# One section for the output projection and the feed-forward of a hybrid attention block, on one Trainium2 core

## The reference

```python
h = rms_norm(x, norm_mix_pre); proj = h @ w_in
out_a = swa_sink_attention(...)            # sliding window, 512 columns
out_b = diff_attention(...)                # two softmax maps, 512 columns
mixed = jnp.concatenate([out_a, out_b], axis=-1) @ w_out
x = x + rms_norm(mixed, norm_mix_post)
h = rms_norm(x, norm_ffn_pre)
f = (jax.nn.silu(h @ w_gate) * (h @ w_up)) @ w_down      # inner width 2816
x = x + rms_norm(f, norm_ffn_post)
```

## Time and profile before

| | us |
|---|---|
| median of 3 executions (2592.71 to 2597.39) | 2595.13 |
| the profiled execution | 2592.32 |
| its span, first to last instruction | 2590.5 |
| PE busy in the span | 2384.5 |
| output projection, first DMA to last hop store issued | 1054.9 to 1299.6 |
| feed-forward, first DMA to the end | 1307.7 to 2590.5 |

### The profile page before, as it was taken

The page is one execution under the profiler, slowest core; times in us unless marked ns, Lnnn a source line. Parts: engine busy times, 40 slices in busy tenths (PEclk is TensorE's granted clock), DMA queues, the critical chain, the costliest instruction groups (busy, mean ns, idle before and its releaser), DMA issues. The chain is left out here.

```text
span 2590.5 us, 36663 instructions
## 1 busy us (share of the span) xinstructions
PE 2384.5 (92%) x11796; PEld 1979.3 (76%) x11796; DVE 1630.0 (63%) x3093; ACT 1203.6 (46%) x2731; POOL 678.1 (26%) x810
## 2 busy tenths in 40 slices
PE   7999997996898888699769999999999999999998
PEld 5888886885777677577558888888888888888886
DVE  5676776554888888433365555556776655554877
ACT  5555564332666666433343333334554333334444
POOL 1223222221566566354401111110000111111001
PEclk9999998997999999899989999999999999999999
DMA  5111122444232221446463323247675333326774
GB/s 175 48 52 50 47 87 67 132 133 155 69 104 71 76 86 37 161 163 222 163 227 113 103 94 114 82 138 245 195 264 195 107 101 106 113 75 221 245 269 146
DMA packets 222105, 340.08 MB, mean 131 GB/s; under 512 B 20320, under 2 KB 119648, under 8 KB 220128
## 3 DMA queue, kind: packets, MB, share of 16 engines
q1 hardware_dynamic: 221920, 337.86, 39.2%
HBM read 234.50 MB, written 103.28 MB: 130 GB/s over the span
## 5 line engine op out<-in xcount | busy, mean ns | idle before, releaser
L2410 PE MATMUL ff_psum<-ff_hop,ff_a_hi 128*128 128x512 f32 x1760 | 542.4, 389 | 4.3 <-issue 4.3
L2410 PEld LDWEIGHTS ff_psum<-ff_hop,ff_a_hi 128*128 128x128 f32 x1760 | 330.0, 188 | 74.4 <-issue 5.9
L2410 PE MATMUL ff_psum<-ff_hop,ff_a_lo 128*128 128x512 f32 x880 | 342.4, 389 | 0.0
L2434 PE MATMUL ff_psum<-ff_a_hi 128*128 128x512 f32 x616 | 239.6, 389 | 0.0
L2434 PE MATMUL ff_psum<-ff_a_lo,ff_a_hi 128*128 128x512 f32 x616 | 239.6, 389 | 0.0
L2434 PE MATMUL ff_psum<-ff_a_hi,ff_a_lo 128*128 128x512 f32 x616 | 239.6, 389 | 0.0
L2073 ACT ACTIVATE ff_a_hi<-ff_w_raw 128x512 fp32r<-128x512 f32 x220 | 138.0, 629 | 212.8 <-PE ff_psum L2410 190.7
L2410 PE MATMUL ff_psum<-hop,ff_a_hi 128*128 128x512 f32 x704 | 219.0, 392 | 17.0 <-DVE ff_a_lo L2186 17.0
L1222 ACT ACTIVATE da_probs<-da_psum,da_bias 128x512 f32<-128x512 f32 (+3 forms) x320 | 195.9, 621 | 74.0 <-DVE da_bias L1274 60.8
L2186 DVE TENSOR_TENSOR ff_a_lo<-ff_w_raw,ff_a_hi 128x512 fp32r<-128x512 f32 x220 | 161.6, 737 | 104.5 <-ACT ff_a_hi L2073 104.5
L2030 POOL TENSOR_TENSOR ff_go<-ff_go 128x512 f32<-128x512 f32 x22 | 28.4, 1290 | 682.8 <-DVE ff_go L2267 682.8
(11 more groups left out here) (235 smaller groups left out, 5350.9 us busy)
## 6 DMA issues: line engine op xcount, KB each, us to landing
g_s<-ff_go SPq DMA_DIRECT2D x154, 256.0 KB, 2.0
ff_ring<-g_s SPq DMA_DIRECT2D x154, 256.0 KB, 2.7
ff_ring<-in_w_down_dram SPq DMA_DIRECT2D x132, 256.0 KB, 3.1
ff_w_raw<-in_w_gate_dram SPq DMA_DIRECT2D x44, 512.0 KB, 3.6
ff_w_raw<-in_w_up_dram SPq DMA_DIRECT2D x44, 512.0 KB, 3.8
pp_x<-in_x_dram SPq DMA_DIRECT2D x32, 512.0 KB, 4.5
hop_s<-op_ht SPq DMA_DIRECT2D x8, 1792.0 KB, 7.5
ff_hop<-hop_s SPq DMA_DIRECT2D x10, 1024.0 KB, 9.2
```

Of the source, the lines that this page charges most:

```text
L2410: last = pe.matmul(ps[:, bank, :], w[:, unit % R, at], hop[i][:, h, c, :], start=(i in (0, 1, 6) and c == 0 and x_ == 0), stop=(c == 3 and ...
L2434: last = pe.matmul(ps[:, bank, :], g[:, unit % R, at], w[:, (unit + 1) % R, :], start=(i in (0, 1, 6) and c == 0 and x_ == 0), stop=(c == ...
```

## The change

`out_proj` and `ffn` become one function, `out_proj_and_ffn`, with one block and no barrier between the two. `OutProj` holds the steps of the output projection, `TailMap` gives every buffer of both a fixed address. Pieces of the two are interleaved by hand:

- SP loads the first four feed-forward weight pieces after k = 8, ACT and DVE split units 0 and 1 after k = 12, DVE makes the sums x = 1, 3, 2 of round 0 after k = 13, and ACT and DVE split units 2 to 5 (on DVE 2 to 4, with the sums x = 4) in tile 15.
- PE runs up-products 0 and 1 straight behind the last `multiply`, then `turn_h(14)`, products 2 to 4, `turn_h(15)`. The rest of the chains of the tiles 14 and 15 stands between the splits of the feed-forward in the same way.
- The hops 2 to 6 lie where buffers of the output projection lay, so their loads wait: 2 and 3 for the last `multiply`, 4 and 5 for `turn_h(15)` and stores, 6 for the last odd store.
- The hop buffer `op_ht` becomes two even ones and one odd one. Even tiles store two blocks, odd tiles five. The two squares share one junk row. The ring of raw output-projection weights has 8 places, not 6.
- The banks of PSUM in the feed-forward swap halves. The `s` buffer becomes four.
- In the phases `pp` and `da`, tensors of 2048 elements or more per partition start at a multiple of 512 bytes; the old rule was 128. All later ones move up by 384 to 1152 bytes.

```diff
-        align = 128 if size >= 128 else 32
+        align = 512 if size >= 2048 else 128 if size >= 128 else 32
```

On SP, within the loop over k and behind it:

```diff
+            if 1 <= k < TILES - 1:
+                (self.store_even if k % 2 == 1 else self.store_odd)(sp, k - 1)
...
+                def between(k):
+                    if k == 8:
+                        sp.wait_ge(op.w_lo_done, 2 * KC)
+                        for u in range(2):
+                            for v in range(2):
+                                load_raw(0, 0, v, u)
+
+                op.sync(sp, between)
+                sp.wait_ge(op.multiplied, 2 * TILES)
+                load_hop(0, 2)
+                load_hop(0, 3)
+                op.store_x(sp, end)
                 for u in range(2):
                     for v in range(2):
                         load_raw(0, 1, v, u)
-                for i in (5, 6):
-                    load_hop(0, i)
+                op.store_even(sp, end - 1)
+                sp.wait_ge(op.h_turned, 2 * TILES)
+                for n in range(2):
+                    sp.wait_ge(op.x_stored[n], 16 * TILES // 2)
+                sp.wait_ge(op.even_stored[0], 32 * TILES // 4)
+                load_hop(0, 4)
+                load_hop(0, 5)
+                op.store_odd(sp, end)
+                sp.wait_ge(op.even_stored[1], 32 * TILES // 4)
+                sp.wait_ge(op.odd_stored, 16 * TILES // 2)
+                load_hop(0, 6)
```

On ACT:

```diff
+                        if n_ == 2:
+                            act.wait_ge(op.multiplied, 2 * end + 1)
...
+                def between(k):
+                    if k == 12:
+                        hi_until(1)
+                    if k == end:
+                        hi_until(5)
...
+                        if p == 0 and g == 2:
+                            hop_half(0, 2, 1)
+                            op.copy_h(act, end - 1)
+                        if p == 0 and g == 5:
+                            op.copy_h(act, end)
                         up_slot(p, j, q)
                         hi_until(UNITS * p + g + 6)
-                        if p == 0 and g in (2, 4, 6, 8, 10):
+                        if p == 0 and g == 1:
+                            hop_half(0, 2, 0)
+                            op.square_x(act, end)
+                        if p == 0 and g in (4, 6, 8, 10):
```

On DVE, and then on PE:

```diff
+                def between(k):
+                    if k == 12:
+                        lo_until(1)
+                    if k == 13:
+                        for x in (1, 3, 2):
+                            for v in range(2):
+                                s_of(0, 0, x, v)
+                    if k == end:
+                        lo_until(3)
+                        for v in range(2):
+                            s_of(0, 0, 4, v)
+                        lo_until(4)
...
+                        if p == 0 and g == 3:
+                            op.norm_x(dve, end)
...
+                            if p == 0 and j == 0 and q in (1, 4):
+                                op.turn_h(pe, end - 1 if q == 1 else end)
```

More of the change, by code:

```diff
@@ L1733 @@
-class FfnMap:
-    def __init__(self, nc, hops):
-        def at(name, shape, offset, dt=F32):
-            return nc.alloc_sbuf_tensor_at(f"ff_{name}", shape, dt, offset=offset)
-        def area(n):
-            return FFN_BASE + AREA * n
-        self.hop = list(hops) + [at(f"hop{n}", [P, 2, 4, HT], area(n), F32R) for n in range(2, 7)]
-        self.keep = at("keep", [P, FC // 2, HT], area(0))
-        self.y_back = at("y_back", [P, 4, D], area(2))
-        self.x_back = at("x_back", [P, 4, D], area(3))
-        self.x_in = at("x_in", [P, 4, D], area(4))
-        self.y2 = at("y2", [P, 4, D], area(5))
-        self.y1 = at("y1", [P, 4, D], area(6))
-        off = area(7)
-        self.w_raw = at("w_raw", [P, 2, 2, 2, D], off)
-        self.ring = at("ring", [P, 16, HT], off)
-        off += 32768
-        self.s1 = at("s1", [P, 2, HT], off)
-        off += 4096
-        self.a_hi = at("a_hi", [P, 7, HT], off, F32R)
-        off += 14336
-        self.a_lo = at("a_lo", [P, 7, HT], off, F32R)
-        off += 14336
-        self.s = at("s", [P, 4, HT], off)
-        off += 8192
-        self.go = at("go", [P, 7, HT], off)
-        off += 14336
-        self.post_row = at("post_row", [P, D], off)
-        off += 4096
-        self.junk = at("junk", [P, D], off, BF16)
-        off += 2048
-        self.half = at("half", [P, 4], off)
-        self.ss = at("ss", [P, 2, 4], off + 32)
-        self.rstd = at("rstd", [P, 4], off + 64)
@@ L1776, in ffn, with out_proj_and_ffn @@
+def out_proj_and_ffn(nc, x, swa_t, mixed, w_out, subln, g_mix, g_ffn, hop_s, x_mid, g_s, y_s, w_gate, w_up, w_down,
+                     g_post, out):
     PAIRS = 2
@@ L1798, in ffn @@
     with ExitStack() as ctx:
-        m = Memory(nc, ctx, "ff")
+        m, om = Memory(nc, ctx, "ff"), Memory(nc, ctx, "op")
         ps = m.psum()
-        b = FfnMap(nc, hops)
+        b = TailMap(nc)
+        op = OutProj(nc, om, ps, b, x, swa_t, mixed, w_out, subln, g_mix, g_ffn, x_mid, hop_s)
+        end = TILES - 1
         hop, keep, ring, w_raw, s1 = b.hop, b.keep, b.ring, b.w_raw, b.s1
@@ L2365, in _ @@
                                 s_of(p, j + 1, 4, v)
-                        if p == 0 and 2 <= g < 12:
+                        if p == 0 and g in (1, 2):
+                            hop_half(0, 2, g - 1)
+                        if p == 0 and 4 <= g < 12:
                             hop_half(0, g // 2 + 1, g % 2)
+                        if p == 0 and g == 5:
+                            op.first_sums(dve, end)
                         if p == 1 and g in (2, 3, 5, 6, 9, 10):
@@ L2467, in hybrid_block @@
     diff_attn(nc, q_s, k_s, v_s, [lambda_q1, lambda_k1, lambda_q2, lambda_k2], mixed)
-    hops = [nc.alloc_sbuf_tensor_at(f"hop{n}", [P, 2, 4, HT], F32R, offset=FFN_BASE + AREA * n) for n in range(2)]
-    with nc.sbuf_tensor("hop_slab", [P, 8320], F32):
-        out_proj(nc, x, swa_t, mixed, w_out, subln, g_mix_post, g_ffn_pre, x_mid, hop_s, hops)
-    ffn(nc, hop_s, hops, x_mid, g_s, y_s, w_gate, w_up, w_down, g_ffn_post, out)
+    out_proj_and_ffn(nc, x, swa_t, mixed, w_out, subln, g_mix_post, g_ffn_pre, hop_s, x_mid, g_s, y_s, w_gate, w_up, w_down,
+                     g_ffn_post, out)
 def rope_table():
```

758 lines of the change are left out of this document (392 added, 366 removed).

## The result

| | before | after |
|---|---|---|
| median of the runs timed side by side, us | 2596.26 (2592.71 to 2597.82, 4 runs) | 2548.52 (2547.37 to 2552.02, 4 runs) |
| the profiled execution | 2592.32 | 2547.37 |
| its span | 2590.5 | 2545.6 |
| PE busy in the span | 2384.5 | 2375.7 |
| first DMA of the output projection | 1054.9 | 1045.1 |

The ratio is 0.9818, 95% interval 0.9806 to 0.983: 47 us less. I had forecast 2566.0, 29 us less, and a range down to 2557.

The account below looks back on a forecast made before the run. PE bounds the kernel from 1353.6 on, so the gain lies in the boundary hole before it. The terms sum to -29.1 us, taking 2595.1 to 2566.0, with a range of 2557 to 2573.

Parts of the forecast that it names:

- Term 7: Buffer addresses in all phases: new starts change nothing on the engines and lose nothing on the DMAs, 0 us.
- My rival: Addresses help: aligned 2 KB packets cut a ninth of first-key and first-load waits, 2 to 3 us, giving 2563.5; chance 0.10.
- Term 4: Start of the output projection: eight ring places bring the second half's weights earlier, -2.5 us (-1 to -3.5).
- Term 1: Boundary from output projection to feed-forward: product 12 starts at 1323.1 instead of 1353.62, -30.5 us.
- the 2.3 before product 10: Within the boundary: PE stalls 2.3 us before product 10, waiting for hop 5's second half.
- landings of 9.2: Boundary with hops 2 to 6 landing in the median 9.2: about -26.5; used in the late-loads rival, chance 0.16.
- Terms 2: Tile 13: six weight sums ahead of norm_y(13) make it late with nothing covering that, +2.7 us (1 to 3.2).
- Term 3: Tile 12: splitting units 0 and 1 there delays norm_y(12), +0.7 us (0 to 1.4).
- Term 6: Clock: one fall of PE's granted clock behind the stalls of about 3 us, +1.7 us (0 to 3.4).
- Term 5: DMA in the output-projection loop: less data ahead removes a PE wait for op_mix_in, -1.2 us.

Follow-up runs that it names:

- e3: Kernel before with only pp's weights moved from 128 past a multiple of 512 bytes onto one; 2590.14 us, ratio 0.9963 to the kernel before.
- e6: Kernel before with pp's stationary operands xt_hi and xt_lo moved from 0 to 128, weights left at 128; 2587.53 us, ratio 0.9971.
- e10: Kernel before with pp's weights at 256 past a multiple of 512 and the stationary operands at 0; 2588.96 us, ratio 0.9971.
- e14: Changed kernel with pp's wv_hi and wv_lo alone 128 bytes past a multiple of 512; 2555.95 us, ratio 0.9847 to the kernel before.
- e5: Changed kernel with 6 places, not 8, in the ring of raw output-projection weights; 2554.91 us, ratio 0.9844 to the kernel before.
- e8: Changed kernel with all buffers of the joint section moved up by 128 bytes; 2550.61 us, ratio 0.9825 to the kernel before.
- e9: Changed kernel with units 0 and 1 split after k = 9, not k = 12; 2549.22 us, ratio 0.9824 to the kernel before.
- e11: Changed kernel with turn_h(15) ahead of product 4, not behind it; 2552.44 us, ratio 0.9836 to the kernel before.
- e12: Changed kernel with the work between output-projection tiles laid only behind odd k; 2550.11 us, ratio 0.9823 to the kernel before.
- e13: Changed kernel with the edits of e12 and e11 together; 2550.27 us, ratio 0.9826 to the kernel before.
- e16: The changed kernel run again, unedited; 2549.70 us, ratio 0.9825 to the kernel before.
- e4_da: Kernel before with the 512-byte alignment rule in da alone; 2596.35 us, ratio 0.9997 to the kernel before.

## Why the prediction missed

- **Term 7, the addresses, is the step that failed.** It said "matmuls and splits of one shape take the same time in both, so I take 0 on the engines". The comparison was between op (starts at 128 and 384, distance 256) and ff (0 and 0), both of the free kind, and I never read the same row of `pp`. It stood in the trace of before: 395 against 389 ns. Of the 9.8 us at T0 the layout gives about 7 (e3, e6, e10, and e14 for half); the other 3 lie within the spread of executions: with the same early code as the changed kernel T0 ran from 1045.1 to 1051.2 in eight profiles (after, e5, e8, e9, e11, e12, e13, e16). My rival had the sign by a mechanism that e4_da does not show; the term was not 0 but about 7.
- **Term 4, the ring, was mis-sized.** I expected DVE's 0.65 to 0.75 a piece to be the next limit and took -2.5, with only the 1.35 us of lost DMA time for the wait. The whole wait of 2.8 and the half clock vanished, -5.4; e5_raw6 brings back 5.1 of it in the stretch.
- **Term 1, the boundary, holds:** -32.3 for -30.5. Stalls of 1.62, 2.94 and 0.65 stand for 2.5, 3.0 and 1.0, the 2.3 before product 10 never came, and 1.9 us of half clock stands behind product 8 (12.78 for 48 matmuls that take 10.9). The last two are one matter: where the clock stayed up PE waited 1.4 before product 10, and product 12 came 0.2 sooner, so I had counted the wait before product 10 too high, by 0.9. Hop 4 landed in 6.05 for my 4.8 to 5.3. (With landings of 9.2 my text has -26.5; its own 4.4 us make it -26.1. No run got there.) The ports behaved as I had laid out from the earlier trace rows: a pair of splits on DVE that takes 1.29 alone (at 1268.25) took 3.48 beside `add_x`. The rule of the Trainium skill that I had named (SBUF — State Buffer, Who interferes with whom) agrees with this.
- **Terms 2, 3 and 6** summed to +5.1 forecast, and tile 13 to the last `multiply` shows +3.8. Term 3 is exact (+0.7). Terms 2 and 6 are not independent, as I had treated them: a fall of the clock at `turn_h(12)` makes PE late, which covers the lateness of `norm_y(13)`. The longer `turn_h(12)` to `turn_m(15)` takes, the shorter `turn_h(13)` waits: 9.22 and 0.54 (after), 7.80 and 1.98 (e16), 6.40 and 2.51 (e11); e5_raw6, with 8.03 and 0.89, lies off this line. Term 6 held one fall at 1.7; there were two, 2.8 and 1.9, and both were in part covered by waits that they took away.
- **Term 5** is -1.9 for -1.2: besides the DMA wait, `turn_h(11)` lost its 0.56. The raw loads at k = 8 cost nothing.
- **The feed-forward** is +1.0 in this profile, with a load of 11.26 us for `ff_ring` on its chain; in e16_after the stretch is 1237.2, so there is nothing to explain beyond 0.3.

Of the 15.8 us between the sum and the spans the layout is 6.8, the spread at T0 3.0, the ring 2.9, the boundary 1.8, term 5 with the loop 1.1, terms 2, 3 and 6 1.3, less 1.0 in the feed-forward. The other 1.7 of the 17.5 between forecast and median is the 2.8 that I added from the profiled execution to the median, which was 1.2 in the changed kernel. Had term 7 been 7 the forecast would have been 2559 and the range 2550 to 2566, with the result still 10 and 1.5 below: the size of term 4 was needed as well. Open is why the distance matters: the traces show the matmul longer and the weight load not, and no run here separates reading the one operand from loading the other.

## What to carry to other kernels

Compare the same instruction across all stages before pricing an address at nothing: a difference of 6 ns in the median, in a row that is not on any wait list, was 7 us of this kernel. For float32r matmuls of 512 columns like these, place the moving and the stationary operand at the same remainder modulo 256 bytes; of the distances tried (0, 128, 256, 384 and 448) only 0 and 256 were free, and the grid did not count. When two stages are joined and a chain over three other engines ends the boundary, count waits ahead of it once and not twice: here an earlier stall, or a fall of the clock, hid in a later one.

## What the runs showed of the hardware that I had not expected

- A float32r matmul of 512 columns whose moving and stationary operands start 128, 384 or 448 bytes apart modulo 512 takes 393 to 395 ns in the median, against 389 at 0 or 256, and PE loses 4.4 ns a matmul. The 256-column ones of `pp_wb_hi` showed no such loss (281 ns before, 283 after).
- The granted clock fell after waits of 2.88 in one execution of a code and stayed up after 2.87 in another (after and e11_turn3, alike up to there), and so did not follow from the length of the wait alone.
- Executions of the same early code differ by up to 6.1 us at T0 (eight profiles), more than any of the edits e9 to e13 moved the section behind it.
